# Six places for the experts' weights instead of four, in the two expert stages of a one-core kernel

## What is computed

```python
def ec_moe(h, w_router, w_gate, w_up, w_down):
    logits = jnp.einsum('bsd,de->bse', h, w_router).astype(jnp.float32)
    aff = jax.nn.softmax(logits, axis=-1)
    gates, idx = lax.top_k(aff.transpose(0, 2, 1), cap)
    xs = jax.vmap(lambda hb, ib: hb[ib])(h, idx)
    g = jnp.einsum('becd,edf->becf', xs, w_gate)
    u = jnp.einsum('becd,edf->becf', xs, w_up)
    y = jnp.einsum('becf,efd->becd', jax.nn.silu(g) * u, w_down)
    y = y * gates[..., None].astype(y.dtype)
    return jax.vmap(lambda ib, yb: jnp.zeros((s, d), yb.dtype).at[ib.reshape(-1)].add(yb.reshape(-1, d)))(idx, y)
```

## Time and profile before

| what | value |
|---|---|
| median of three runs | 3887.81 us |
| span of the profiled execution | 3884.4 us |
| TensorE matmul busy | 3578.4 us (92%) |
| VectorE busy | 2522.3 us (65%) |
| ScalarE busy | 1854.0 us (48%) |
| DMA | 607.63 MB, mean 156 GB/s over the span |
| VectorE, low halves of experts' weights (L4459) | 96 x 4.43 us |
| ScalarE, high halves of experts' weights (L4365) | 96 x 3.63 us |
| granted TensorE clock, mean | 0.969 of full |

### The profile page before, as it was taken

How to read it: one execution, slowest core, us unless ns; L and a number is a source line. 1 busy time by engine, 2 the same in 40 slices (tenths; PEclk the granted TensorE clock), 3 DMA queues, 4 the chain that set the end, 5 groups by cost and what they waited for, 6 DMA issues and landing times. The chain is left out here.

```text
span 3884.4 us, 57831 instructions
## 1 busy us (share of the span) xinstructions
PE 3578.4 (92%) x23078; PEld 2954.4 (76%) x23078; DVE 2522.3 (65%) x3931; ACT 1854.0 (48%) x2531; POOL 255.5 (7%) x178
## 2 busy tenths in 40 slices
PE   7999999999999999999999995999888999976996
PEld 5778888777777888877997784777787877765774
DVE  4477673498767667666325645778665766547776
ACT  4224432287334444443215742677436766533775
POOL 0000000000000000000000000233000000002342
PEclk9999999999999999999999997999899999998998
DMA  5011225532513337752413232899623130135998
GB/s 208 28 50 60 87 71 189 187 121 85 182 60 139 149 141 287 261 207 89 145 45 131 62 141 104 329 365 368 200 52 117 37 131 29 48 133 207 366 366 283
DMA packets 229433, 607.63 MB, mean 156 GB/s; under 512 B 30456, under 2 KB 130600, under 8 KB 211136
## 3 DMA queue, kind: packets, MB, share of 16 engines
q1 hardware_dynamic: 212896, 546.91, 38.4%
q0 software_dynamic: 13168, 55.16, 5.0%
q10 hardware_dynamic: 3120, 2.10, 0.2%
HBM read 483.38 MB, written 120.73 MB: 156 GB/s over the span
## 5 line engine op out<-in xcount | busy, mean ns | idle before, releaser
L4459 DVE TENSOR_TENSOR ring_r<-ring,oN_r 128x4096 fp32r<-128x4096 f32 x48 | 212.5, 4427 | 64.5 <-ACT oN_r L4365 64.5
L4459 DVE TENSOR_TENSOR ring_r<-ring,hT_r 128x4096 fp32r<-128x4096 f32 x48 | 212.3, 4424 | 62.1 <-ACT hT_r L4365 62.1
L4365 ACT ACTIVATE hT_r<-ring 128x4096 fp32r<-128x4096 f32 x48 | 174.0, 3630 | 73.1 <-DMA ring<-in_w_all 72.9
L4365 ACT ACTIVATE oN_r<-ring 128x4096 fp32r<-128x4096 f32 x48 | 174.1, 3630 | 68.0 <-DMA ring<-in_w_all 67.2
L171 PE MATMUL scans_G<-ring_r 128*128 128x512 f32 x512 | 204.6, 400 | 0.0
L1433 DVE CUSTOM_DVE_ANT_0 oN<-heads_scores,heads_table 128x1024 f32<-128x1024 f32 x128 | 156.1, 1220 | 42.5 <-issue 42.5
L173 PE MATMUL scans_G<-ring_r 128*128 128x512 f32 x448 | 175.1, 391 | 0.0
L172 PE MATMUL scans_G<-hT_r,ring_r 128*128 128x512 f32 x448 | 175.0, 391 | 0.0
L4237 POOL TENSOR_TENSOR moe_taker<-moe_zero 128x1 f32<-128x1 f32 x64 | 136.5, 2133 | 433.7 <-ACT moe_y L4444 394.0
L1388 ACT ACTIVATE oN<-oN,heads_nm 128x1024 f32<-128x1024 f32 x128 | 146.7, 1146 | 23.4 <-DVE heads_nm L1433 20.2
L172 PE MATMUL mlp_ps<-mlp_room_r,ring_r 128*128 128x512 f32 x384 | 150.4, 392 | 0.0
(11 more groups left out here) (805 smaller groups left out, 10523.0 us busy)
## 6 DMA issues: line engine op xcount, KB each, us to landing
ring<-in_w_all SPq DMA_DIRECT2D x110, 2048.0 KB, 19.1
hidden_operands<-mlp_room SPq DMA_DIRECT2D x56, 512.0 KB, 2.6
ring<-in_w_mlp SPq DMA_DIRECT2D x38, 512.0 KB, 5.5
ring<-in_w_mlp SPq DMA_DIRECT2D x8, 2048.0 KB, 8.1
ring<-in_w_all SPq DMA_DIRECT2D x12, 1024.0 KB, 6.4
branch_gates<-scans_stg SPq DMA_DIRECT2D x48, 256.0 KB, 2.0
merge_raw<-branch_gates SPq DMA_DIRECT2D x16, 768.0 KB, 5.1
ring<-hidden_operands SPq DMA_DIRECT2D x22, 512.0 KB, 3.5
```

The costliest lines, as they stand in the source:

```text
L4365: act.activation(w_high[n % RING], buf[:, (first + n) % RING, :], ACT.Copy).then_inc(w_cast, 1)
L4459: dve.tensor_tensor(buf_r[:, b, :], buf[:, b, :], w_high[n % RING].bitcast(F32), ALU.subtract)\
```

## The change

The experts' stage no longer takes its 48 places from the ring alone. It takes the four that the ring holds already, and then runs six places of its own for raw and low halves: the ring's four, a new tensor `more` of one place, and the first half of `hT`. The high halves keep three places (both halves of `oN_r`, and the second half of `hT_r`). SyncE loads place 4 at the start of the stage and place 5 when both halves of the logits are done (that is when `hT` has been read), and after that place n+6 when product n is done. ScalarE counts a semaphore `w_used` where it counted `slots_free`. The cast of place 3 moves from before the choice of tokens to behind the first gate, because there are three places of high halves now. The small tensors of the routing (`lt`, `work`, `aff`, `wr_wide`, `best`, `vals`, `idx`, `ex`) lie inside `y` and `sg`, which the loop uses only later. The next stage's first place is fed when product 42 is done.

```diff
+        DEEP, HIGHS, EARLY = 6, 3, RING
+        first = m["ring"].take(EARLY)
+        first_row = first + m["ring"].shift
+        m["ring"].skip(3 * NE - EARLY)
...
+        more, more_r = twin_buffer(nc, st.ctx, f"moe{layer}_more", [P, SLOT])
...
-        w_high = [m[t_][:, h_ * NT // 2:(h_ + 1) * NT // 2, :].rearrange("p t n -> p (t n)")
-                  for t_ in ("oN_r", "hT_r") for h_ in range(2)]
+        w_raw = [buf[:, (first + j) % RING, :] for j in range(RING)] + [more[:], half_of("hT", 0)]
+        w_low = [buf_r[:, (first + j) % RING, :] for j in range(RING)] + [more_r[:], half_of("hT_r", 0)]
+        w_high = [half_of("oN_r", 0), half_of("oN_r", 1), half_of("hT_r", 1)]
...
+        flat_y = y[:, :, :].rearrange("p b n -> p (b n)")
+        lt = flat_y[:, 0:S]
...
         @block.sync
-            m["ring"].feed(sp)
+            for n in range(EARLY, DEEP):
+                if n == DEEP - 1:
+                    sp.wait_ge(logits, 2)
+                sp.dma_start(w_raw[n], m["w_all"][first_row + n, :, :]).then_inc(w_in[n], 16)
+            with sp.Fori(0, 3 * NE // DEEP - 1) as i:
+                for n in range(DEEP):
+                    sp.wait_ge(w_used, i * DEEP + (n + 1))
+                    sp.dma_start(w_raw[n], m["w_all"][bass.ds(i * DEEP + (first_row + DEEP + n), 1), :, :]
+                                 .rearrange("o p n -> (o p) n")).then_inc(w_in[n], 16)
             if keep_last:
+                sp.wait_ge(w_used, 3 * NE - DEEP + 1)
+                m["ring"].feed(sp)
...
         @block.scalar
             def cast(i, n):
-                m["ring"].wait(act, first + n, i, SLOTS)
-                act.activation(w_high[n % RING], buf[:, (first + n) % RING, :], ACT.Copy).then_inc(w_cast, 1)
+                if n < EARLY:
+                    m["ring"].wait(act, first + n)
+                else:
+                    act.wait_ge(w_in[n % DEEP], i * (SLOTS // DEEP * 16) + 16 * (n // DEEP + (n % DEEP >= EARLY)))
+                act.activation(w_high[n % HIGHS], w_raw[n % DEEP], ACT.Copy).then_inc(w_cast, 1)
...
             cast(0, 2)
-            cast(0, 3)
...
             gate(0, 0)
             take_x(0, 1, 0)
+            cast(0, 3)
             up(0, 0)
...
         @block.vector
-                dve.tensor_tensor(buf_r[:, b, :], buf[:, b, :], w_high[n % RING].bitcast(F32), ALU.subtract)\
+                dve.tensor_tensor(w_low[n % DEEP], w_raw[n % DEEP], w_high[n % HIGHS].bitcast(F32), ALU.subtract)\
```

More of the change, by code:

```diff
@@ L4142, in moe_stage @@
         TURNS = NE // EJ
-        first = m["ring"].take(3 * NE)
+        DEEP, HIGHS, EARLY = 6, 3, RING
+        first = m["ring"].take(EARLY)
+        first_row = first + m["ring"].shift
+        m["ring"].skip(3 * NE - EARLY)
         LAST = NE - 1
[L4145 to L4154, removed]
+        wr = m["wr"]
+        more, more_r = twin_buffer(nc, st.ctx, f"moe{layer}_more", [P, SLOT])
         xs = st.sb("xs", [P, EJ, D])
@@ L4159, in moe_stage, with half_of @@
         buf, buf_r = m["ring"].buf, m["ring"].buf_r
-        w_high = [m[t_][:, h_ * NT // 2:(h_ + 1) * NT // 2, :].rearrange("p t n -> p (t n)")
-                  for t_ in ("oN_r", "hT_r") for h_ in range(2)]
-        y = st.sb("y", [P, 2, D])
+        def half_of(name, h_):
+            return m[name][:, h_ * NT // 2:(h_ + 1) * NT // 2, :].rearrange("p t n -> p (t n)")
+        w_raw = [buf[:, (first + j) % RING, :] for j in range(RING)] + [more[:], half_of("hT", 0)]
+        w_low = [buf_r[:, (first + j) % RING, :] for j in range(RING)] + [more_r[:], half_of("hT_r", 0)]
+        w_high = [half_of("oN_r", 0), half_of("oN_r", 1), half_of("hT_r", 1)]
+        y = st.sb("y", [P, 2, D])
+        mx, add_up = st.sb("mx", [P, NT]), st.sb("add_up", [P, NE])
+        sel, first_wins = st.sb("sel", [P, 4, NE]), st.sb("first_wins", [P, NE])
+        gates, rows = st.sb("gates", [P, NE]), st.sb("rows", [P, NE], U32)
+        flat_y = y[:, :, :].rearrange("p b n -> p (b n)")
+        lt = flat_y[:, 0:S]
+        work = flat_y[0:64, S:S + HALF]
+        aff = flat_y[:, S + HALF:S + 3 * HALF // 2].rearrange("p (t e) -> p t e", e=64)
+        wr_wide = flat_y[:, S + 3 * HALF // 2:2 * S].rearrange("p (k e) -> p k e", e=32)
+        best = sg[0:64, 0, 0:2 * CAP].rearrange("p (b n) -> p b n", b=2)
+        vals, idx = sg[0:64, 0, 2 * CAP:3 * CAP], sg[0:64, 0, 3 * CAP:4 * CAP].bitcast(U32)
+        ex = sg[:, 1, 0:NT * NE].rearrange("p (t e) -> p t e", e=NE)
         taker, zero, zeroed = st.sb("taker", [P, 2 * NE + 1]), st.sb("zero", [P, 1]), st.sem("zeroed")
@@ L4174, in moe_stage @@
         xs_in, add_up_in = [st.sem(f"xs_in{b}") for b in range(EJ)], st.sem("add_up_in")
+        w_in, w_used = [st.sem(f"w_in{p_}") for p_ in range(DEEP)], st.sem("w_used")
         L = G[:, 0, 0:NT * NE].rearrange("p (t e) -> p t e", e=NE)
@@ L4180, in moe_stage @@
         if keep_last:
-            tokens, y_high, y_low, gain = last_rows(m, (first + 3 * NE - 2) % RING)
+            tokens, y_high, y_low, gain = last_rows(m, (first + 2) % RING)
             token_ids, mark, ids_in = st.sb("token_ids", [P, S]), st.sb("mark", [P, 1]), st.sem("ids_in")
@@ L4196, in w_views @@
         def w_views(n, k):
-            high, low = w_high[n % RING], buf_r[:, (first + n) % RING, :]
+            high, low = w_high[n % HIGHS], w_low[n % DEEP]
             return [v.rearrange("p (k n) -> p k n", k=k) for v in (high, low)]
@@ L4363, in cast @@
             def cast(i, n):
-                m["ring"].wait(act, first + n, i, SLOTS)
-                act.activation(w_high[n % RING], buf[:, (first + n) % RING, :], ACT.Copy).then_inc(w_cast, 1)
+                if n < EARLY:
[3 more added lines that the diff above has]
+                act.activation(w_high[n % HIGHS], w_raw[n % DEEP], ACT.Copy).then_inc(w_cast, 1)
+            for _ in range(EARLY):
+                m["ring"].release(act)
             cast(0, 0)
@@ L4374, in _ @@
             act.wait_ge(aff_T, 1)
-            act.activation(work[:], Y[0:64, 0, :], ACT.Copy).then_inc(work_in, 1)
+            act.activation(work, Y[0:64, 0, :], ACT.Copy).then_inc(work_in, 1)
             cast(0, 2)
-            cast(0, 3)
             act.wait_ge(sel_in, 1)
@@ L4400, in gate @@
                 act.wait_ge(g_done, i * EJ + (j + 1))
-                m["ring"].release(act)
+                act.nop().then_inc(w_used, 1)
                 act.wait_ge(gu_free, i * EJ + (j + 1))
@@ L4456, in low @@
             def low(i, n):
-                b = (first + n) % RING
                 dve.wait_ge(w_cast, i * SLOTS + n + 1)
-                dve.tensor_tensor(buf_r[:, b, :], buf[:, b, :], w_high[n % RING].bitcast(F32), ALU.subtract)\
+                dve.tensor_tensor(w_low[n % DEEP], w_raw[n % DEEP], w_high[n % HIGHS].bitcast(F32), ALU.subtract)\
                    .then_inc(w_split, 1)
```

## The result

The changed kernel takes 3850.84 us (3850.05 to 3852.66) against 3888.08 (3887.11 to 3892.68) before, median of four runs each: a ratio of 0.990, 95% interval 0.989 to 0.991. A second set of runs gave 3849.6 us and the same 0.990 (0.989 to 0.992). So 37 us were gained where 16 were forecast.

The account below looks back on a forecast made before the run. The prediction took full transfer engines to bound the experts' loops. Gains of 22.4 us from the bodies, less 5.4 for the moved cast and 1.2 for the clock, gave about -16 us: median 3872 us, range 3850 to 3888, forecast's own 3860 to 3880.

Parts of the forecast that it names:

- This is the price of the transfers: Experts' loops: the old pace of 19.85 and 20.08 us per body is the transfers' cost, 20.0 us per expert.
- A queue that seldom runs empty: Experts' loops: loads asked for six products ahead make places cheaper; bodies become 19.2 us, 22.4 us less in both stages.
- my 5.34 and 4.84: Weights' queue: us of transfer time per place as things were, and at the best rate of 433 GB/s.
- at best: Transfers in the loops: 18.5 us per expert at the best rate, 3 x 4.84 + 4.0.
- The 0.9 us for gathers: Loop bodies: average wait of TensorE for late gathered rows, 0.9 us added to each of 12 bodies.
- The 0.4 us for small waits: Loop bodies: 0.4 us added to each for the clock and small waits in VectorE's tight order.
- TensorE's own pace: Rival for the loops: gathers come in time, 13 bodies take 233 us, 48 us gained, 3840 us; chance 0.12, nearness included.
- the 9.7 us in hand: Loops: loads held ahead cover 0.6 us x 13 bodies with nothing left over, an argument against bodies at TensorE's speed.
- second way: Loops: a place still costs 5.34 us, pace stays, only the lead is gained: 2 x 10.7 - 5.4 = 16.0 us.
- The cast of place 3, moved: Each stage's opening: the later cast delays product G1 by 2.7 us per stage, -5.4 us of the gain.
- the clock, -1.2: Opening, behind TensorE's 4.3 us pause: lost clock of 1.2 us, once for both stages, bounds 0 and 2.4.
- The rule on HBM: Transfers in the loops: if about 358 GB/s per core is the limit, only the lead is gained, still -16 us.

Follow-up runs that it names:

- Experiment 1: The changed kernel with four places again instead of six, everything else of the change kept: 3903.72 us, 1.003 of the kernel before the change.
- 8: The kernel before the change without the loops' scatter-adds, so the experts' results are not added to the rows: 3843.79 us, 0.988.
- 6: Gather of expert e+4 issued ahead of the scatter-add of expert e: on the kernel before the change 3893.74 us, 1.001; on the changed kernel 3882.86 us, 0.998.
- experiment 4: The changed kernel with VectorE's low half of place 3 moved last and places 4 and 5 loaded only after products 0 and 1: 3842.51 us, 0.989.
- 5: The changed kernel with each load waiting for one product more, as with five places: 3860.0 us, 0.992 of the kernel before the change.
- after: The changed kernel itself, with six places, against the kernel before the change: 3850.84 us, 0.990.
- experiment 2: The changed kernel with places 4 and 5 asked for only when products 0 and 1 are done: 3848.48 us, 0.989 of the kernel before the change.
- Experiment 3: The changed kernel with VectorE's low half of place 3 moved behind silu(g)*u and the second rows' low half in the prologue: 3833.51 us, 0.986.

## Why the prediction was right and wrong

The direction was right and 3850.84 lies inside the range, at its lower end; the size was not: 37 us, more than twice the forecast, and outside the 3860 to 3880 that was given as the forecast's own range. Two terms failed, in opposite directions.

**What set the old pace.** "This is the price of the transfers" was the wrong reading. The share is the time that packets took, and it stayed at 1.00 while the rate rose from 369 to 389 GB/s. As the rows have it, the limit was the round of one place. From the trace of the kernel before, in time order: a cast, the load asked for when the product with it is done, and the cast of what that load brought.

```profile
2538.34 3.63 ACT L4365 ACTIVATE hT_r<-ring 128x4096 fp32r<-128x4096 f32 x1 [3.46 <-DMA ring<-in_w_all]
...
2548.71 0.48 PE L171 MATMUL moe_u_ps<-hT_r,moe_x_high 128*128 128x512 f32 x1
...
2554.65 0.33 SPq L140 DMA_DIRECT2D ring<-in_w_all  x1
...
2564.26 3.63 ACT L4365 ACTIVATE hT_r<-ring 128x4096 fp32r<-128x4096 f32 x1 [1.89 <-DMA ring<-in_w_all]
```

From the cast to the product that uses it 10.4 us (cast and low half are 8.1 of them), to the next request 5.9, to the cast of the new load 9.6: 25.9 us for four places, 6.5 us for a place and 19.4 for an expert. Both casts waited for their load, and so did the three between them. At 17.8 us for an expert, 5.9 for a place, six places allow 35 us for the round, so that a load may take 17.2 us and harm nobody. Experiment 1 shows that the number of places is the cause, 8 that room in the transfer engines does not by itself bring TensorE's pace, 6 that the gathers did not set it. That the round is what connects these is read from the rows; no run changed the length of cast or product alone.

**"A queue that seldom runs empty".** The price of a place fell to 5.01 us, between my 5.34 and 4.84, and the transfers need 18.4 us for an expert, close to the 18.5 "at best" (experiment 4). The 0.9 us for gathers failed: 0.6 us were waited in a whole stage, not 0.9 in each of 12 bodies. I carried over the lateness of the gathers of before, where they were issued behind results that came in an uneven rhythm. The 0.4 us for small waits was near 0 too. The two terms make 31.2 of the 33.1 us by which the bodies beat the forecast. Without both terms the sum is TensorE's own pace, the rival that had a chance of at most 0.12: 233 us were worked out for it, 231.7 and 231.9 measured. The argument against it, that the 9.7 us in hand "cover 0.6 us x 13 bodies, but with nothing left over", was right in substance: they cover 0.7 us x 13, and experiments 4 and 5 show the pace of the transfers as soon as there is less in hand. The gathers of after are on time, though by little: they land 21.4 us behind the results, and TensorE comes to their transposes 22.1 us behind them in most bodies. Before, it came there after 22.1 to 25.8 us. The even rhythm leaves 0.7 us; why single gathers of before took longer was not traced.

**The "second way"**, by which the pace stays and only the lead is gained, is refuted by the bodies of 17.8 us and by experiment 2: without the lead the kernel is as fast. That two ways gave -16 looked like support; it was a coincidence.

**"The cast of place 3, moved"**, -5.4, and the clock, -1.2. The mechanism was right: the wait before G1 is 4.33 and 4.32 us, 4.3 was worked out. The price was too small, 12.3 us and not 6.6. Some 2.4 us in the first stage are G1 at half clock, where I had taken 1.2 once for both stages from a window at 0.88; and G0 was itself in part at half clock (0.61 us a matmul in the rows above), which I had not foreseen. In the second stage G0 ran at half clock in the kernel before too (a window of it below), which fits the smaller loss there, 5.1 and not 7.2 us. Experiment 3 gives the loss back: 12.7 us by expert 0 in the two stages. The two profiled spans differ by 18.8 us; another 4.4 of these are the earlier start of the first stage (2366.57, and 2370.92 in after), behind code that is the same in both.

So the sum of the two stages should have been 55.5 - 12.3 = 43.2, and reads 22.4 - 6.6 in the forecast. The 8.1 us that were lost elsewhere stood in no term of it.

**The rule on HBM** (the Trainium skill, DMA: Bandwidth & Descriptors, section Specifications, about 358 GB/s for a core) is not borne out here as a limit: the loops move 396 to 398 GB/s for 200 us. The page's figure is half of what it gives for two cores together, and this kernel runs on one. By that rule an expert's 7.34 MB would need an estimated 20.5 us, and the bodies take 17.8.

## What to carry to other kernels

A DMA share of 1.00 does not prove that the transfers are the limit: compare the GB/s with the best stretch of the same kernel, and follow one buffer round (cast, product, request, landing). If the round divided by the number of buffers is the pace, one buffer more helps without a byte less to move, until the transfers themselves set the pace. In a hand-written prologue, ask of each instruction that is moved what stands behind it in the order of the next engine: here one line moved on VectorE is worth some 16 us. And a lead in loads is worth something only where nothing else lets the loads catch up.

## What the runs showed of the hardware

- **The clock.** After a pause of TensorE of 4.33 us the granted clock was 0.52 for some 5 us (matmuls of 512 columns 0.63 us instead of 0.39); after 0.15 us (experiment 3) and 1.63 us (before) in the same place it was 1.00. But product G0, behind the same wait of 1.46 us in both kernels and both stages, ran at full clock in the first stage of before, and for some 3 us at half clock in its second stage and in both stages of after. A pause alone does not tell; what else counts stayed open. Before, at the start of G0 of the second stage:

```profile
3533.00:3536.00 3.00, 3.00 (x9) 2.27 (x8) 3.00 (x1) 0.00 (x0) 0.00 (x0) 0.52 0.01 4
```

- **Requests in flight.** A 2 MB load took 9 to 12 us from request to cast with four places (before, five loads from 2540 us on), 10.6 us to its landing in experiment 1 (median of 29), and 17.2 us with six (median of 21). The rate was 369 GB/s in before, 373 in experiment 1 and 396 in after (2480 to 2680): a longer queue bought 6 to 7% of rate for over half as much time again for each load.
- **Indirect DMAs in one queue.** In after a scatter-add of 0.5 MB lands after 12.7 us and a gather after 13.3 (medians). With the gather issued first, the scatter-add takes 16.5 and the gather 9.4: the second in the queue pays. DMA issues of after in 2500 to 2690 (KB each, median us to landing):

```profile
ring<-in_w_all SPq DMA_DIRECT2D x21, 2048.0 KB, 17.2
...
moe_xs<-h_rows,moe_rows POOLq DMA_INDIRECT x11, 13.3
x_rows<-moe_y,moe_rows POOLq DMA_INDIRECT x10, 12.7
```
